# A router that works tile by tile, and experts that gather raw residual rows: one change to a fused two-block kernel

## The reference

```
h2 = rmsnorm(x, ffn_norm)
group_logits  = h2 @ w_rg + b_rg            # 4 groups, take the best
expert_logits = h2 @ w_re + b_re            # 32 experts, 8 in each group
top 2 of the 8 in the best group            # weights: g1 * softmax(top 2)
y = sum over the 2 experts e of  weight_e * ((silu(h2 @ w_gate[e]) * (h2 @ w_up[e])) @ w_down[e])
out = rmsnorm(x + y, final_norm)
```

## Time and profile before

| | us |
|---|---|
| median of 3 runs | 1565.99 (1565.85 to 1566.46) |
| profiled execution, its own time | 1568.27 |
| its span, first to last instruction | 1566.5 |
| PE busy | 1484.0 (95 %) |
| DVE busy | 530.9 (34 %) |
| ACT busy | 462.5 (30 %) |
| POOL busy | 325.6 (21 %) |

### The profile page before, as it was taken

How to read it: one execution, slowest core, us unless ns; L and a number is a source line. 1 busy time by engine, 2 the same in 40 slices (tenths; PEclk the granted TensorE clock), 3 DMA queues, 4 the chain that set the end, 5 groups by cost and what they waited for, 6 DMA issues and landing times.

```text
span 1566.5 us, 17027 instructions
## 1 busy us (share of the span) xinstructions
PE 1484.0 (95%) x6571; PEld 770.7 (49%) x6571; DVE 530.9 (34%) x1131; ACT 462.5 (30%) x955; POOL 325.6 (21%) x351
## 2 busy tenths in 40 slices
PE   5998899999999999999999999999999599999997
PEld 2676554444676454444676444454455433333332
DVE  0164310566543230476442201232144512121225
ACT  1232531221755252231764121232232201111112
POOL 1020110444000120356000000004432233333410
PEclk7999899999999999999999999999999699999999
DMA  9556033331030211211010322111400789999995
GB/s 352 194 211 253 1 108 124 118 108 54 1 111 1 97 54 54 81 54 54 1 55 1 108 78 84 54 54 54 166 1 28 298 350 383 413 387 375 414 410 224
DMA packets 85112, 233.77 MB, mean 149 GB/s; under 512 B 16816, under 2 KB 24758, under 8 KB 70824
## 3 DMA queue, kind: packets, MB, share of 16 engines
q1 hardware_dynamic: 69986, 204.00, 34.7%
q0 software_dynamic: 13824, 24.98, 4.3%
q10 hardware_dynamic: 1222, 3.70, 0.6%
HBM read 266.39 MB, written 16.80 MB: 181 GB/s over the span
## 4 chain that ended last, share of the span: by engine, by line
PE 87%; DVE 3%; ACT 3%; issue 3%; DMA 2%; POOL 1%; SPq 0%; DVEq 0%; POOLq 0%; ACTq 0%
PE PS L1854 17%; PE PS L2281 11%; PE PS L2020 9%; PE PS L2086 7%; PE PS L2307 6%; PE PS L1934 5%; PE PS L1831 4%; PE PS L2084 4%; PE PS L2185 4%; PE PS L1956 3%; PE PS L1944 3%; PE PS L2129 2%; DMA RING<-in_w_mod_dram 1%; PE PS L2156 1%; PE PS L2270 1%
## 5 line engine op out<-in xcount | busy, mean ns | idle before, releaser
L1854 PE MATMUL PS<-RH,RING 128*128 128x512 f32 (+1 forms) x864 | 317.5, 524 | 3.4 <-DMA RING<-in_w_in_dram 3.4
L1854 PEld LDWEIGHTS PS<-RH,RING 128*128 128x128 f32 x864 | 163.5, 191 | 148.6 <-issue 136.1
L2020 PE MATMUL PS<-RING,RY 128*128 128x512 f32 x320 | 139.5, 592 | 0.0
L2281 PE MATMUL PS<-RING,RM 128*64 128x512 f32 x384 | 114.6, 598 | 2.8 <-DVE RM L1682 2.8
L1328 DVE SCALAR_TENSOR_TENSOR RM<-RM,COL 128x512 f32<-128x512 f32 (+1 forms) x180 | 114.1, 701 | 0.1
L2086 PE MATMUL PS<-RH,RING 128*128 128x512 f32 x256 | 114.1, 594 | 0.0
L1370 DVE TENSOR_REDUCE SMALL<-PS 128x1 f32<-128x768 f32 (+1 forms) x80 | 67.9, 848 | 131.4 <-PE PS L1934 131.3
L637 POOL TENSOR_SCALAR SMALL<-SMALL 128x1 f32<-128x1 f32 (+1 forms) x32 | 9.9, 309 | 468.6 <-ACT WS L867 225.4
L1934 PE MATMUL PS<-RK,RH 96*128 96x256 f32 (+1 forms) x288 | 106.2, 488 | 1.1 <-ACT WS L1014 0.7
L2020 PEld LDWEIGHTS PS<-RING,RY 128*128 128x128 f32 x320 | 60.0, 190 | 71.3 <-issue 71.3
L639 POOL TENSOR_TENSOR SMALL<-SMALL 128x1 f32<-128x1 f32 (+2 forms) x54 | 56.5, 1046 | 87.3 <-DVE SMALL L1302 84.7
(11 more groups left out here) (368 smaller groups left out, 2248.2 us busy)
## 6 DMA issues: line engine op xcount, KB each, us to landing
RING<-in_w_in_dram SPq DMA_DIRECT2D x18, 2048.0 KB, 8.0
RING<-in_w_mod_dram SPq DMA_DIRECT2D x12, 2048.0 KB, 9.0
RING<-in_w_expert_gate_dram SPq DMA_DIRECT2D x19, 1024.0 KB, 10.2
RING<-in_w_expert_up_dram SPq DMA_DIRECT2D x19, 1024.0 KB, 12.6
RING<-in_w_out_dram SPq DMA_DIRECT2D x8, 2048.0 KB, 8.2
RK<-in_w_expert_down_dram SPq DMA_DIRECT2D x8, 1024.0 KB, 8.4
X<-in_w_expert_down_dram SPq DMA_DIRECT2D x8, 1024.0 KB, 11.8
WS<-in_w_expert_down_dram SPq DMA_DIRECT2D x8, 1024.0 KB, 8.7
```

The source lines that it names most:

```text
L1854: last = mm(o[:, 0:T], w[:, k, m * P:(m + 1) * P], HT[:, k, 0:T], start=(k == 0), stop=(k == 7))
L2020: last = mm(PS[:, j % 2, :], YT[:, k, t * P:(t + 1) * P], w[:, k, :], start=(k == 0), stop=(k == 7))
L2281: last = mm(PS[64 * z:64 * z + 64, n % 2, :], XGT[n % 2][:, k, 64 * z:64 * z + 64], free(GU[n % 3][z], [2048, 2], [1, DE], off=DE * k), st ...
```

## The change

- **Router by tile.** `choose(n, part)` finds group, experts, one-hots and sums of one tile as soon as its logits are there. `ranks(n)` on PE (bank 6 or 0) and `places(n, tiles)` on DVE follow for that tile, then `main_slots(n)` on PE (bank 7), with a third value beside the two row numbers: rs of the row in that place. The group logits stand behind the expert logits now, and the eight logits of the group are no longer picked out: the others get -1e30 and all 32 go into the maximum.
- **The last projection is split.** `output2(15)` runs in two halves with `router_logits(2)` and `router_turn(3, 0)` between them.
- **Main and overflow apart.** The 16 main columns of SLOT are written right after `main_slots(3)`, and gathers 0 to 3 wait for that alone. The overflow arithmetic follows on DVE; `overflow_slots` on PE stands behind `gate_up(0)` and `turn_tile(1)`, `overflow_rows` on DVE between `tile_turned(0)` and `tile_turned(1)`, `last_tables` behind `tile_turned(1)`. The tables LAST are turned one behind `gate_up(1)` and one behind `gate_up(2)`. POOL waits for the overflow slots ahead of gather(4).
- **Raw rows.** ACT stores X itself (`store_rows`), two of the tiles still within the attention loop. The norms of these rows (DVE L1258, ACT L1168) are gone. `turn_tile` reads every eighth column of the gathered rows. rs of each place (RSL) is the scale of silu, and a factor of `product`.
- **Loads.** The downs of tile 1 (2 MB), and of the third tile the first expert's gate (1 MB) and the second expert's gate and up (2 MB), are loaded during the attention. The first expert's up follows behind the first `turn_tile`. The final norm's weights (0.5 MB) are loaded with tile 6 instead of ahead of the experts. Buffers are moved to make room.

```diff
+load_down(1)
 sp.wait_ge(p_pv2, 16)
 load_down(0)
 sp.wait_ge(p_w, 24)
 load_gate_up(0)
+first_third = TILE_PAIRS[2][1] * 2
+sp.dma_start(GU[2][0][:, 0:2048], wg[first_third]).then_inc(w_gu[2], 16)
+sp.wait_ge(v_mx2, 64)
+load_gate_up(2, (1,))
 sp.wait_ge(p_o.sem, p_o.through(4))
 load_gate_up(1)
-load_gate_up(2, (0,))
-sp.wait_ge(d_xn, 16 * 4)
-load_gate_up(2, (1,))
-sp.wait_ge(p_ss2, 8)
-sp.dma_start(GB[:, :], bass.AP(a["final_norm_2"].tensor, 0, [[0, P], [1, D]])).then_inc(d_fw, 16)
-sp.wait_ge(p_sl, 1)
-sp.wait_ge(v_wr, 2)
 sp.wait_ge(m_xt, 1)
-load_down(1)
+sp.dma_start(GU[2][0][:, 2048:4096], wu[first_third]).then_inc(w_gu[2], 16)
 for n in range(3, NP):
     sp.wait_ge(m_gu, n - 2)
     load_gate_up(n)
+    if n == 6:
+        sp.wait_ge(v_wr, 2)
+        sp.dma_start(GB[:, :], bass.AP(a["final_norm_2"].tensor, 0, [[0, P], [1, D]])).then_inc(d_fw, 16)
     if n - 1 >= 2:
         sp.wait_ge(m_dn, 2 * (n - 2))
...
 g.wait_ge(v_wr, 1)
+g.wait_ge(v_sl, 2)
 g.wait_ge(m_xt, 1)
 gather(4)
...
+def store_rows(n):
+    t = 3 - n
+    act.wait_ge(v_o.sem, v_o.at(4, 9 + 2 * n))
+    act.dma_start(xn_d.rearrange("(t p) d -> p t d", p=P)[:, t, :], X[:, 2 + t, :]).then_inc(d_xn, 16)
...
-    A(SG[n % 2], PS[:, n % 2, 0:DE], ACT.Silu).then_inc(m_sg, 1)
+    A(SG[n % 2], PS[:, n % 2, 0:DE], ACT.Silu, scale=RSL[:, place_column(n):place_column(n) + 1]).then_inc(m_sg, 1)
...
+def choose(n, part):
+    t = 3 - n
+    seen = RM[:, LOGITS + 64 * t:LOGITS + 64 * t + 40]
+    masked = RM[:, SCRATCH + 64 * t:SCRATCH + 64 * t + 32]
+    if part == 0:
+        v.wait_ge(v_l, n + 1)
+        link(v.max(words(t, 8, 8), seen[:, 32:40]))
+        link(v.max_index(words(t, 16, 8).bitcast(U32), words(t, 8, 8), seen[:, 32:40]))
+        link(v.tensor_copy(words(t, 24, 1), words(t, 16, 1).bitcast(U32)))
+        link(v.tensor_scalar(words(t, 28, 4), IOTA[:, 0:4], words(t, 24, 1), 1.0, ALU.is_equal, ALU.subtract))
+        link(v.scalar_tensor_tensor(free(masked, [8, 4], [1, 8]), free(words(t, 28, 4), [1, 4], [0, 8]), -NEG,
+                                    free(seen, [8, 4], [1, 8]), ALU.mult, ALU.add))
+    else:
+        link(v.max(words(t, 40, 8), masked))
+        link(v.max_index(words(t, 48, 8).bitcast(U32), words(t, 40, 8), masked))
+        link(v.tensor_copy(words(t, 56, 2), words(t, 48, 2).bitcast(U32)))
+        one = ONEHOT[:, 64 * t:64 * t + 64]
+        link(v.tensor_tensor(free(one, [32, 2], [1, 32]), free(IOTA, [0, 2], [1, 32]), free(words(t, 56, 2), [1, 2], [0, 32]),
+                             ALU.is_equal))
+        own = SUMS[:, 32 * t:32 * t + 32]
+        last = v.tensor_tensor(own, one[:, 0:32], one[:, 32:64], ALU.add)
...
+        last.then_inc(v_lg, 1)
+        for c in range(2):
+            v.tensor_tensor(free(VTM, [96, 2], [48, 2], [1, 16], off=192 * t + 16 * c), free(one, [32, 2], [1, 2], [2, 16]),
+                            free(VAL, [1, 2], [0, 2], [0, 16], off=8 * c + 2 * t), ALU.mult)
+        v.tensor_scalar(free(VTM, [96, 2], [48, 2], [1, 16], off=192 * t + 32), free(one, [32, 2], [1, 2], [2, 16]),
+                        rs[:, t:t + 1], None, ALU.mult)
+
+def places(n, tiles_):
+    t = 3 - n
+    w = 2 * tiles_
+    v.wait_ge(p_rk, n + 1)
+    link(v.tensor_tensor(free(PRD, [32, w], [1, 32], off=64 * t), free(ONEHOT, [32, w], [1, 32], off=64 * t),
+                         free(PS[:, 0 if n == 1 else 6, :], [32, tiles_], [0, 2], [1, 32], off=32 * t), ALU.mult))
+    link(v.tensor_reduce(RANK[:, 2 * t:2 * t + w], free(PRD, [32, w], [1, 32], off=64 * t), AX, ALU.add))
+    v.tensor_tensor(free(OHM, [64, w], [1, 64], off=128 * t), free(I64, [0, w], [1, 64]),
+                    free(RANK, [1, w], [0, 64], off=2 * t), ALU.is_equal).then_inc(v_pos, 1)
...
 router_rows(0)
 residual2(13)
 mean_square(7)
...
 router_rows(1)
 logits(0)
+choose(0, 0)
+choose(0, 1)
 residual2(14)
+logits(1)
 router_rows(2)
+choose(1, 0)
+choose(1, 1)
+places(0, 1)
 residual2(15)
+logits(2)
+choose(2, 0)
 router_rows(3)
+choose(2, 1)
+places(1, 1)
 logits(3)
+choose(3, 0)
+choose(3, 1)
+places(3, 2)
...
 
+v.wait_ge(p_sl, 1)
+v.tensor_scalar(free(SLOT[:, :], [24, 2], [1, 16]), free(PS[:, 7, :], [16, 2], [1, 16], off=256), float(NONE), None, ALU.add).then_inc(v_sl, 1)
+
...
+def overflow_rows():
+    link(v.tensor_tensor(free(ENDS, [32, OVER], [1, 32]), free(INC, [0, OVER], [1, 32]), free(IOTA, [1, OVER], [0, 32]), ALU.is_le))
+    link(v.tensor_reduce(ENDED, free(ENDS, [32, OVER], [1, 32]), AX, ALU.add))
+    v.scalar_tensor_tensor(WROW[:, :], ENDED, float(P), free(TOKF, [0, OVER]), ALU.mult, ALU.add).then_inc(v_wr, 1)
+    v.wait_ge(p_sl, 2)
+    v.tensor_copy(RSL[:, 16:24], PS[:, 7, 320:328])
+    v.tensor_scalar(free(SLOT[:, :], [24, 2], [1, 8], off=16), free(PS[:, 7, :], [8, 2], [1, 8], off=304), float(NONE), None,
+                    ALU.add).then_inc(v_sl, 1)
+
...
-    v.tensor_tensor(free(HE[n % 2], [P, 2], [1, P]), halves(SG[n % 2]), halves(PS[:, n % 2, :], DE), ALU.mult).then_inc(m_he, 1)
+    r = RSL[:, place_column(n):place_column(n) + 1]
+    v.scalar_tensor_tensor(free(HE[n % 2], [P, 2], [1, P]), halves(PS[:, n % 2, :], DE), r, halves(SG[n % 2]), ALU.mult,
+                           ALU.mult).then_inc(m_he, 1)
...
 tile_turned(0)
+overflow_rows()
 tile_turned(1)
+last_tables()
...
+def ranks(n):
+    t = 3 - n
+    pe.wait_ge(v_lg, n + 1)
+    own = SUMS[:, 32 * t:32 * t + 32]
+    before = SUMS[:, 96:128] if n == 1 else SUMS[:, 64 + 32 * n:96 + 32 * n]
+    at = PS[:, 0 if n == 1 else 6, 32 * t:32 * t + 32]
+    last = mm(at, BEFORE, own, start=True, stop=(n == 0))
+    if n >= 1:
+        last = mm(at, ONES, before, start=False, stop=True)
+    last.then_inc(p_rk, 1)
+
...
+def main_slots(n):
+    t = 3 - n
+    for k in range(2):
+        j = 2 * t + k
+        for z in range(2):
+            last = mm(PS[64 * z:64 * z + 64, 7, 256:304], OHM[:, 64 * j:64 * j + 64], VTM[:, 96 * j + 48 * z:96 * j + 48 * z + 48],
+                      start=(n == 0 and k == 0), stop=(n == 3 and k == 1))
+    if n == 3:
+        last.then_inc(p_sl, 1)
+
+def overflow_slots():
+    pe.wait_ge(v_pos, 4)
+    for j in range(8):
+        for z in range(2):
+            last = mm(PS[64 * z:64 * z + 64, 7, 304:328], OHF[:, 64 * j:64 * j + 64], VTF[:, 48 * j + 24 * z:48 * j + 24 * z + 24],
+                      start=(j == 0), stop=(j == 7))
+    last.then_inc(p_sl, 1)
+
...
 router_turn(2, 1).then_inc(p_rt, 1)
+ranks(0)
+output2(15, range(2))
+router_logits(2)
 router_turn(3, 0).then_inc(p_rt, 1)
+output2(15, range(2, 4))
+ranks(1)
+pe.wait_ge(v_pos, 1)
+main_slots(0)
+router_logits(3, range(4))
 router_turn(3, 1).then_inc(p_rt, 1)
+router_logits(3, range(4, 8))
+ranks(2)
+pe.wait_ge(v_pos, 2)
+main_slots(1)
+ranks(3)
+totals()
+pe.wait_ge(v_pos, 3)
+main_slots(2)
+main_slots(3)
...
-        last = tr(PS[:, 4 + k // 4, (k % 4) * P:(k % 4 + 1) * P], XG[n % 4][:, k * P:(k + 1) * P], IDENT)
+        last = tr(PS[:, 4 + k // 4, (k % 4) * P:(k % 4 + 1) * P], free(XG[n % 4], [8, P], off=k), IDENT)
...
 turn_tile(0)
 gate_up(0)
 turn_tile(1)
+overflow_slots()
 for n in range(NP):
     if n + 1 < NP:
         gate_up(n + 1, range(8) if n + 2 < NP else range(4))
+    if n < 2:
+        turn_last(n)
     turn_hidden(n)
     if n + 2 < NP:
```

More of the change, by code:

```diff
@@ L1194, in rows @@
                     A(YO[n % 3][:, 512:1024], PS[:, 3, :], ACT.Copy).then_inc(m_yv, 1)
-            act.wait_ge(p_la, 1)
-            for z in range(2):
-                last = A(LAST_T[z], PS[:, 6 + z, :], ACT.Copy)
-            last.then_inc(a_la, 1)
             half_tile(0)
@@ L1597, in _ @@
-            for t in range(4):
-                last = v.tensor_tensor(free(PRD, [8, 4], [1, 8], off=32 * t), free(RM[:, LOGITS:LOGITS + 256], [8, 4], [1, 8], off=64 * t + 4),
-                                       free(SCR, [1, 4], [0, 8], off=4 * t), ALU.mult)
-            link(last)
-            link(v.tensor_reduce(tiles(ROUTE, [1, 8], off=32), free(PRD, [32, 4], [1, 8], [8, 4]), AX, ALU.add))
-            for t in range(4):
-                last = v.max(words(t, 40, 8), words(t, 32, 8))
-            link(last)
@@ L1605, in _ @@
-            for t in range(4):
-                last = v.max_index(words(t, 48, 8).bitcast(U32), words(t, 40, 8), words(t, 32, 8))
-            link(last)
-            link(v.tensor_copy(EID([1, 2]), tiles(ROUTE, [1, 2], off=48, dt=U32)))
-            link(v.scalar_tensor_tensor(EID([1, 2]), tiles(ROUTE, [0, 2], off=24), 8.0, EID([1, 2]), ALU.mult, ALU.add))
-            for k in range(2):
-                last = v.tensor_tensor(free(ONEHOT, [64, 4], [1, 32], off=32 * k), free(IOTA, [0, 4], [1, 32]),
-                                       tiles(ROUTE, [0, 32], off=56 + k), ALU.is_equal)
@@ new lines, in last_tables @@
+            def last_tables():
+                v.wait_ge(a_lg, 1)
+                total = free(SCR, [1, 4], [1, 1], off=40)
+                link(v.tensor_scalar(total, tiles(EXPS, [1, 1], off=10), 1.0, None, ALU.add))
```

(22 more changed lines are left out.)

207 lines of the change are left out of this document (78 added, 129 removed).

## The result

| | before | after |
|---|---|---|
| median, 20 runs each | 1566.01 us (1561.41 to 1569.46) | 1569.36 us (1567.12 to 1573.26) |
| ratio | | 1.0025, 95% interval 1.0016 to 1.0034 |
| profiled execution: time, span | 1568.27, 1566.5 us | 1569.32, 1567.5 us |
| first router turn on PE, from the start | 1203.8 us | 1200.7 us |
| from there to the end of the span | 362.65 us | 366.85 us |

What follows compares the result with a forecast made beforehand. The prediction saw PE as the bound, with a 26.6 us hollow between router logits and first expert product. Terms -8.6 + 2.0 + 1.3 + 1.2 = -4.1 gave 1562 us, range 1556 to 1578.

Steps and rivals of the forecast that it cites:

- Term 1: Router to first expert product: gate/up(0) starts at 1243.2 instead of 1251.82, -8.6 us, bounds -5 to -10.
- D: Loads during the attention: if all 5 MB counted (12 us), time near 1552; chance 0.03.
- Rival C: Gathers take 5.2 us as before, or the last store holds them, each 2 us: about 1564.5; chance 0.12.
- Term 2: Behind the first tile, overflow products and small DVE steps delay the next tile: +2.0 us, bounds 0.8 to 3.
- Term 3: Two turns of the last tables on PE and the ACT copy during early experts: +1.3 us, bounds 0.9 to 2.
- Rival A: Strided reads double the transposes of 24 tiles, 20.9 us on PE: +11, 1577; chance 0.27.
- Rival B: Strided transposes have a small cost, 0.2 ns an element: -0.4, 1565.6; chance 0.08.
- Term 4: Final norm weights (0.5 MB) at tile 6 lengthen the stall before down(8): +1.2 us, bounds 0 to 1.2.

Runs made afterwards that it cites:

- loads_old: Changed kernel with the 5 MB of early loads put back behind the attention, as in the kernel before: 1572.36 us, ratio 1.0045.
- third_turn1: Changed kernel with final norm weights loaded at tile 3 and, on DVE, tile 1's scaling ahead of the wait for overflow slots: 1561.34 us, ratio 0.9964.
- after_again: The changed kernel run once more, nothing altered: 1571.2 us, ratio 1.0035.
- before_gb6: Kernel before, with only the load of the final norm weights (0.5 MB) moved to tile 6: 1573.84 us, ratio 1.0054.
- gb_third: Changed kernel with the final norm weights loaded at tile 3 instead of tile 6: 1561.79 us, ratio 0.9984.
- gb_last: Changed kernel with the final norm weights loaded behind the last down weights instead of at tile 6: 1561.89 us, ratio 0.9982.
- gb_five: Changed kernel with the final norm weights loaded at tile 5 instead of tile 6: 1562.9 us, ratio 0.999.
- gb_twelve: Changed kernel with the final norm weights loaded at tile 12 instead of tile 6: 1564.76 us, ratio 1.0005.
- gb_half: Changed kernel with the final norm weights loaded in two halves of 64 partitions, at tiles 3 and 6: 1569.85 us, ratio 1.0022.
- hold_down8: Changed kernel with one added wait: PE holds tile 8's down product until tile 10's gate and up have landed: 1565.47 us, ratio 0.9995.
- three failed repairs: Changed kernel variants: tile 19's down rows issued earlier, 1581.68 us; last two overflow tiles exchanged, 1565.6; overflow tiles at places 8 and 11 exchanged, 1566.64.

## Why the prediction was wrong, step by step

**Term 1, -8.6, measured -7.3: right in mechanism.** The router part came out to a tenth: the slot cast at rt+31.4 instead of rt+37.2, 5.8 us earlier, 5.85 forecast. That isn't luck, since the steps hold too: residual2(15) ends at rt+20.1 (20.2 forecast), logits(3) at rt+25.6 (25.6), places(3) at rt+30.2 (30.1). The gather is off. I took 3.4 us to its landing and it takes 4.74 with the load queue empty. It isn't a matter of traffic any more: in the DMA's row from 1233 to 1239 (0.15 us a slice) nothing moves for 1.8 us behind its issue at 1233.28.

```profile
DMA  7410000000000009992554699998423845489856
```

loads_old confirms what was said under D, that the early megabytes buy an idle queue for the gather and no more: 4.6 us at gate/up(0), not 12. Rival C is answered: the first gather starts 1.2 us behind the cast, no store holds it; its landing has 1.3 of C's 2.

**Term 2, +2.0, measured +1.2**, from 1.36 to 2.59 us; the products take 1.07 and not 1.5. third_turn1 takes it away. **Term 3, +1.3, measured some 0.9**: 0.59 twice, less what the hidden turn saves behind them; down(0) waits for nothing. That makes -5.2, and -4.6 was measured at down(1): gate/up(0) itself, in part at the low clock, took 9.56 us and not the 9.04 of the kernel before, a cost in none of my terms. How long the low clock holds there differs between profiles of one kernel, too: after_again has 8.45 us for gate/up(0) but 8.78 for gate/up(1), and is 4.2 us ahead at down(1). Forecast was -5.3.

**Rival A, 0.27, refuted.** The period is 11.70 and eight turns take 0.88 us, read with a step as they are. The rule on SBUF lines of 16 bytes (the Trainium skill, "Advanced Engine Details and Errata", section Memory Cachelines) is visible in the weight load, 188 against 140 ns, though not as a doubling; PE hides it. Rival B falls with it.

**Term 4 is the step that failed.** "0.5 MB / 412 GB/s = 1.2 us more of it", with 0 to 1.2 as bounds. At the measured rate the 1.2 us are right for the bytes. But I priced a load in a saturated stretch as added length of the next stall. Measured, the stalls around tile 8 became shorter, 3.6 us without low clock (1.87, 1.01, 0.73) against 2.96 and 1.65 of low clock, and the price came 130 us later: 9.7 us at down(19) in the trace; 9.3 us in before_gb6 by the medians (8.4 by the ratio), and here the difference between 1569.36 and the 1561.8 of gb_third, 7.6 (6.4 by the ratios). Where the load is out of the way, my sum without term 4, -5.3, can be set against gb_third (-2.7 by the medians, -3.3 by the ends; its stall before down(8) is 3.35 and not 2.96, with 1.21 more before gate/up(8)). For third_turn1, which has no term 2 either, the sum would be -7.3; it has -3.8 by the medians and -5.2 by the ends. So the direction was right without term 4, and the size too large. What I had in hand and didn't use was the state of each later load. I looked at where PE waits, and not at what was nearly late: down(19)'s rows landed 4.7 us before need, late in a saturated stretch. Still, the margin alone would not have told it: 1.2 us of load are less than 4.7. Nor is PE's lead to blame, since it moves the issue of the rows and the need for them alike: third_turn1 comes to down(19) 5 us ahead of the kernel before and has its rows 5.4 us ahead of need. What failed is the step from bytes to time: a load behind the dry point can take away the slack behind tile 8, and then two late pieces come 12 us behind the others. No row of the kernel before showed me that delay growing, so its size could not have been forecast from them.

What stays open: why some pieces fall behind, and the more the longer the saturation lasts, though not evenly (the gather of 1432.5 has 5.6 us between the 8.9 and the 12.1). The profile's page shows 16 KB packets of an instruction queue (q8, 53 of them, 0.2% of 16 engines), some 1 us each; if all went through one engine they would delay it, but no row names the engine. The Trainium skill ("DMA: Bandwidth & Descriptors", section Latency and other measured facts) says that two of the 16 engines are usually the slower ones in traces, and guesses at GpSimd's descriptor rings. That fits here as far as the traces go: the late pieces are those of loads that GpSimd issued (up to 13.5 us behind the first nine tenths), while SP's at the same time have their last piece 2.2 to 2.5 us behind the first nine tenths. It fits only in part: one piece in sixteen is late here and not two, and the guess itself no run here tests. Also open is what puts single runs of gb_last, gb_five and gb_twelve among the longer ones, and how much slack is enough (1.6 us was, in third_turn1, and 1.1 was not, in gb_half); start-up differences of some microseconds are the only thing seen to vary.

## What to carry to other kernels

In a stretch where the DMA is saturated, don't price an added load by its bytes alone. Look for the point at which the queues next run dry: ahead of it 0.5 MB were free here, within what the runs can tell. Behind it, list every later load up to the next such point with its margin, and ask which short drain the added load would fill; compare the last piece of each landing with the rest, since it was the last piece that fell behind. A wait that gives the DMA time to drain can be worth more than it costs (hold_down8), and in the three failed repairs the loss moved to another tight load. Compare profiles from a mark just ahead of the change, since their starts differ by more than the effect sought.

## What the runs showed of the hardware

- Pieces of GpSimd's loads drift apart while the DMA is saturated: in after the last of 32 pieces landed 12 us behind the first 30, some 110 us after tile 8 had passed without slack; in the kernel before no piece was over 2.1 us behind the one before it among the gathers, nor over 2.0 in down(19)'s rows. Where the DMA drains whole, about one engine is busy at the end for 1.2 us (hold_down8) to 2.7 us (after, from 1500).
- 0.5 MB can switch a kernel between two times 8 us apart, with few runs between (none in gb_half), at mean granted clocks of 0.974 to 0.986 over all runs of gb_half and gb_twelve.
- PE's weight load of a tile with a step of 32 bytes: 188 ns against 140, and eight transposes take 0.88 us against 0.87.
- An indirect gather of 128 rows needed 4.7 us from issue to landing on an idle DMA, of which 1.3 us are GpSimd's own instruction.
